# Residual update and next norm by halves of the tokens in a two-layer diffusion block

## The chip, the cores and the metric

One NeuronCore of a Trainium2 chip runs the whole program in one launch. The metric is device time in microseconds (us). TensorE is called PE below, VectorE DVE, ScalarE ACT, GpSimd POOL, and SP is the engine that issues most loads.

## The reference

Two layers (DEPTH = 2) act on 256 latent tokens `x` and 256 context tokens `ctx`, each 1024 wide, in float32. Each layer has three sublayers, and each of these takes the residual stream `h`, normalises it, applies a product, normalises the result and adds it:

```python
def modulate(x, g, shift, scale):
    return rms_norm(x, g) * (1.0 + scale) + shift

def ffn_sublayer(x, shift, scale, gate, g_pre, g_post, wg, wu, wd):
    y = swiglu(modulate(x, g_pre, shift, scale), wg, wu, wd)
    return x + FFN_RES * gate * rms_norm(y, g_post)
...
        h = ffn_sublayer(h, mod[:, 0], ...)          # and hc, with the context's own shift, scale, gate
        y, yc = token_mixing(modulate(h, g[2], ...), modulate(hc, g[2], ...), ...)
        h = h + mod[:, 5] * rms_norm(y, g[3])        # and hc, if another layer follows
        h = ffn_sublayer(h, mod[:, 6], ...)
```

`rms_norm` takes its mean over the 1024 features of one token, so a norm needs the whole of the residual of its tokens, but of no others. `D_FF` is 2816. `token_mixing` projects to 21 tiles of 128 columns, runs window attention, a gated linear attention (gla) and an mLSTM, and projects back with `w_out`.

## The kernel before

**Layout.** Features lie on the 128 partitions and tokens on the free axis: `H[128, 8, 512]` is the residual, with the latents in columns 0 to 255 of each of its KT = 8 feature tiles and the context in 256 to 511. The normed input is held as a high and a low part, `u_hi` and `u_lo`, the FFN's middle as `ht_hi` and `ht_lo`, the weights as `w_hi` and `w_lo`. `products` issues three matmuls for each product of two such pairs (L324, L325, L326), with up to 512 tokens each. In the second layer the part behind the mixer has latents alone, so all its operations have 256 tokens.

**Weights.** The weights come in 182 units, in the order of their use. Unit n uses slot n % 2 of `raw`, `w_hi` and `w_lo`. SP loads it, ACT writes `w_hi` (`split_hi`, L300, waits for the load and for `unit_used`: PE must be done with unit n-2), DVE writes `w_lo` (`split_lo`, L308), and PE waits for `lo_ready` (`begin`). A unit of gate and up weights holds 128 columns of each (48 products of 512 tokens). An output tile of `down` has two units of 11 feature blocks each, 33 products apiece; it is accumulated in bank 4 or 5 in turn. A unit of `project_out` holds two output tiles.

**Between two products.** There are five places where one sublayer ends and the next begins; z counts the sublayers from 0 to 5. At each, all of the following runs between the last product of one and the first of the next:
- ACT squares the last output tile (L724) and copies it with its gate to `Y_ffn` or `Y_mix` (L729, `post_tile`); the squares of the first seven tiles were added up by DVE (L1075).
- PE sums the squares over the partitions with a column of ones (L1617), ACT takes the root (L662), DVE the reciprocal (L984), PE spreads it over the partitions (L1624).
- DVE scales each tile of Y (L1086) and adds it to H (L1094), 8 tiles; ACT squares each new tile of H (L687), PE sums them (L1617), then root, reciprocal and spread again.
- for each of the 8 tiles DVE scales H (L1005), ACT applies the modulation (L696) and copies to `u_hi` (L700), DVE subtracts to `u_lo` (L1000), and PE's first unit of the next product takes tile k as soon as `u_ready` says so. In this stretch ACT and DVE also split the next product's second unit.

The order on each engine is that of the code: each engine's program is written out by hand, with semaphores between them. In three of the FFN products DVE also sums columns of a 512-wide matrix for later layers' modulation (`ada_sums`, L1025 and L1034), four instructions at a time, between its own steps.

## Time and profile before

| what | value |
|---|---|
| time, median of 3 runs (lowest, highest) | 2001.98 us (1999.55, 2007.71) |
| time of the profiled execution | 2008.94 us |
| its span, first to last instruction | 2007.1 us |
| PE busy with matmuls | 1873.5 us, 93% |
| DVE busy | 1109.3 us, 55% |
| ACT busy | 760.1 us, 38% |
| POOL busy | 243.6 us, 12% |
| mean granted clock of PE, share of full | 0.953 |

The profiled execution has 1.8 us around its span. PE is the busy engine, and its clock is at its full level (2.4 GHz) save for a few stretches at half of it (1.2 GHz). The places at which PE is not busy, and where its clock falls, are those between two products, and parts of the mixer. How busy an engine is on the whole tells little there: within such a place it matters which engine is waited for last.

### The profile page before, as it was taken

What the parts mean: (1) busy time and instruction counts of PE and PEld (TensorE: products, weight loads), DVE (VectorE), ACT (ScalarE), POOL (GpSimd) and SP (SyncE); (2) the same over time, 40 slices, a digit from 0 to 9 for tenths busy, and PEclk for the clock granted to TensorE, in tenths of its full rate; (3) what the DMA queues carried; (4) which work ended last, traced back from release to release, by engine and by line L of the source; (5) the groups of instructions that cost most, each with busy time, mean ns of one, the idle gap of its engine ahead of it and who ended that gap; (6) DMA issues with size and microseconds to landing.
All of it is one profiled execution on the core that took longest, in us unless ns stands there. A gap on an engine that the chain in (4) does not pass through costs nothing. (4 is left out here: it accounts for less than half of the span.)

```text
span 2007.1 us, 25666 instructions
## 1 busy us (share of the span) xinstructions
PE 1873.5 (93%) x10461; PEld 1521.9 (76%) x10461; DVE 1109.3 (55%) x1630; ACT 760.1 (38%) x1132; POOL 243.6 (12%) x327
## 2 busy tenths in 40 slices
PE   5999999979998886999999979999999799879998
PEld 3788877857786664888778858887888488769997
DVE  1777722245756646777522267775222676855544
ACT  4423222236436445222313253222232645654443
POOL 4011110012531000111110001110000152000000
PEclk7999999989999797999999979999999799979999
DMA  9566654342321022666553416665234243036654
GB/s 298 147 180 196 178 160 141 96 113 43 85 64 43 11 63 63 202 178 191 168 173 87 115 49 202 178 194 153 79 94 113 65 106 84 13 105 165 178 166 122
DMA packets 366469, 254.05 MB, mean 127 GB/s; under 512 B 30610, under 2 KB 343276, under 8 KB 366352
## 3 DMA queue, kind: packets, MB, share of 16 engines
q1 hardware_dynamic: 345648, 182.97, 33.1%
q0 software_dynamic: 20704, 69.44, 10.8%
q8 instruction: 83, 1.36, 0.3%
q14 instruction: 34, 0.28, 0.0%
HBM read 251.30 MB, written 1.07 MB: 126 GB/s over the span
## 5 line engine op out<-in xcount | busy, mean ns | idle before, releaser
L324 PE MATMUL bank<-u_hi,w_hi 128*128 128x512 f32 (+2 forms) x1872 | 690.8, 369 | 29.7 <-DVE u_lo L1000 20.6
L325 PE MATMUL bank<-u_lo,w_hi 128*128 128x512 f32 (+2 forms) x1872 | 682.8, 365 | 0.0
L326 PE MATMUL bank<-u_hi,w_lo 128*128 128x512 f32 (+2 forms) x1872 | 682.5, 365 | 0.0
L308 DVE TENSOR_TENSOR w_lo<-raw,w_hi 128x2048 fp32r<-128x2048 f32 (+2 forms) x182 | 373.0, 2049 | 262.3 <-ACT w_hi L300 262.1
L324 PEld LDWEIGHTS bank<-u_hi,w_hi 128*128 128x128 f32 (+1 forms) x1872 | 357.8, 191 | 110.8 <-issue 51.6
L326 PEld LDWEIGHTS bank<-u_hi,w_lo 128*128 128x128 f32 (+1 forms) x1872 | 357.5, 191 | 56.8 <-issue 0.9
L325 PEld LDWEIGHTS bank<-u_lo,w_hi 128*128 128x128 f32 (+1 forms) x1872 | 358.1, 191 | 53.8 <-issue 0.5
L300 ACT ACTIVATE w_hi<-raw 128x2048 fp32r<-128x2048 f32 (+2 forms) x182 | 311.8, 1713 | 144.0 <-PE bank L326 126.6
L324 PE MATMUL bank<-ht_hi,w_hi 128*128 128x512 f32 (+1 forms) x704 | 256.8, 365 | 1.4 <-DVE w_lo L308 1.4
L326 PE MATMUL bank<-ht_hi,w_lo 128*128 128x512 f32 (+1 forms) x704 | 255.3, 363 | 0.0
L325 PE MATMUL bank<-ht_lo,w_hi 128*128 128x512 f32 (+1 forms) x704 | 255.2, 363 | 0.0
L715 ACT ACTIVATE tmp_a<-bank 128x512 f32<-128x512 f32 (+1 forms) x88 | 47.9, 544 | 537.1 <-PE bank L326 537.1
L1034 DVE SCALAR_TENSOR_TENSOR ada_sum<-ada_slot,silu_c,ada_sum 128x512 f32<-128x512 f32 x336 | 230.7, 746 | 0.0
L512 POOL DMA_DIRECT2D ada_slot<-in_ada_w_dram x128 | 92.1, 720 | 936.3 <-DVE ada_sum L1034 655.1
L1053 DVE TENSOR_TENSOR tmp_b<-bank,tmp_a 128x512 f32<-128x512 f32 (+1 forms) x88 | 55.0, 625 | 210.9 <-ACT tmp_a L715 210.9
L324 PEld LDWEIGHTS bank<-ht_hi,w_hi 128*128 128x128 f32 x704 | 132.8, 189 | 27.6 <-issue 6.7
L326 PEld LDWEIGHTS bank<-ht_hi,w_lo 128*128 128x128 f32 x704 | 132.8, 189 | 20.7
L325 PEld LDWEIGHTS bank<-ht_lo,w_hi 128*128 128x128 f32 x704 | 132.9, 189 | 20.4
L724 ACT ACTIVATE tmp_a<-bank 128x512 f32<-128x512 f32 (+1 forms) x48 | 25.3, 527 | 206.6 <-PE bank L326 206.6
L1075 DVE TENSOR_TENSOR tmp_b<-tmp_b,tmp_a 128x512 f32<-128x512 f32 (+1 forms) x36 | 21.7, 604 | 124.0 <-ACT tmp_a L724 124.0
L1056 DVE TENSOR_TENSOR ht_lo<-tmp_b,ht_hi 128x512 fp32r<-128x512 f32 (+1 forms) x88 | 55.1, 626 | 56.7 <-ACT ht_hi L717 56.7
L717 ACT ACTIVATE ht_hi<-tmp_b 128x512 fp32r<-128x512 f32 (+1 forms) x88 | 50.9, 578 | 61.1 <-DVE tmp_b L1053 61.1
(244 smaller groups left out, 1486.4 us busy)
## 6 DMA issues: line engine op xcount, KB each, us to landing
ada_slot<-in_ada_w_dram POOLq DMA_DIRECT2D x128, 512.0 KB, 4.7
...
```

The lines of the kernel that those rows point to most:

```text
L300: nc.scalar.activation(w_hi[s][:, 0:size], raw[s][:, 0:size], ACT.Copy).then_inc(hi_ready[s], 1)
L308: nc.vector.tensor_tensor(w_lo[s][:, 0:size], raw[s][:, 0:size], w_hi[s][:, 0:size].bitcast(F32), ALU.subtract).then_inc(lo_ready[s], 1)
L324: nc.tensor.matmul(acc, wh, xh, start=first, stop=False)
L325: nc.tensor.matmul(acc, wh, xl, start=False, stop=False)
L326: return nc.tensor.matmul(acc, wl, xh, start=False, stop=last)
L512: pool.dma_start(ada_slot[slot][:], src[:, 2 * r:2 * r + 2, b * BLOCK:(b + 1) * BLOCK]).then_inc(ada_loaded[slot], 16)
L715: nc.scalar.activation(tmp_a[j][:, 0:T], bank[2 * j][:, 0:T], ACT.Silu).then_inc(gated["silu_ready"], 1)
L717: nc.scalar.activation(ht_hi[:, f, 0:T], tmp_b[j][:, 0:T], ACT.Copy).then_inc(gated["hthi_ready"], 1)
L724: nc.scalar.activation(tmp_a[b][:, 0:T], bank[4 + b][:, 0:T], ACT.Square).then_inc(post["ysq_ready"], 1)
L1034: ins = nc.vector.scalar_tensor_tensor(acc[:], ada_slot[slot][:, kk, :], c_k, acc[:], ALU.mult, ALU.add)
L1053: nc.vector.tensor_tensor(tmp_b[j][:, 0:T], bank[2 * j + 1][:, 0:T], tmp_a[j][:, 0:T], ALU.mult).then_inc(gated["prod_ready"], 1)
L1056: nc.vector.tensor_tensor(ht_lo[:, f, 0:T], tmp_b[j][:, 0:T], ht_hi[:, f, 0:T].bitcast(F32), ALU.subtract).then_inc(gated["ht_ready"], 1)
```

## The change

At the first four of the five places (z < HALVED = 4) the work is done for the latents first and then for the context, 256 tokens at a time, and PE's products are cut the same way and put between the steps:
- the last output tile of the sublayer (`last_tile`) is computed for the latents in bank 5, then for the context in bank 6. Between the context's products PE sums the latents' squares, spreads their reciprocal and sums the squares of their new H;
- the first two weight units of the next product (`halved_gate_up`, or four output tiles in `project`) are computed for the latents, then for the context, again with the context's sums between the products. In `project` the tiles 0 to 3 now use four banks;
- ACT and DVE have one sequence each for the whole place (`halved_norm`), in which the latents' norm and the context's residual update alternate (`last_half` squares and copies one half of the last tile, `half_root` takes a root, `u_part` waits for `u_ready`). The splits of the next product's units are placed within it: the first unit's split, which was in `down`, and the second's;
- at the end of `project_out`, ACT has a semaphore of its own for tile 6 (`six_done`).
The counts of the semaphores change with it (`posts`, `norms`); POOL's waits for `ss_done` now wait for the context's half. The work behind z = 4, for latents alone, stays as it was.

```diff
+            def halved_norm(z, Y, n_last):
+                layer, q = (z + 1) // 3, (z + 1) % 3
+                act.wait_ge(post["ysq_added"], (KT - 1) * z + KT - 2)
+                act.wait_ge(post["lat_done"], z + 1)
+                last_half(Y, z, 0)
+                half_root(POST_SUMS, 0, 0, post["ss_done"], post["ss_rms"], posts(z) + 1)
+                if z == 1:
+                    unit_done(act, n_last, 0, 2, 0)
+                    last_half(Y, z, 1)
+                for k in range(KT):
+                    if k == KT // 2 and z != 1:
+                        split_hi(act, second_unit(layer, q) - 1)
+                    half_square(z, 0, k)
+                if z != 1:
+                    unit_done(act, n_last, 0, 2, 0)
+                    last_half(Y, z, 1)
+                half_root(NORM_BANKS[0], 0, 1, norm["sq_used"], norm["rms_ready"], KT * norms(z + 1) + KT)
+                half_root(POST_SUMS, 1, 0, post["ss_done"], post["ss_rms"], posts(z, 1) + 1)
+                for k in range(KT):
+                    half_mod(z, 0, k)
+                    if k == KT // 2 + 1:
+                        split_hi(act, second_unit(layer, q))
+                    if k >= KT // 2:
+                        half_square(z, 1, k - KT // 2)
+                for k in range(KT // 2, KT):
+                    half_square(z, 1, k)
+                half_root(NORM_BANKS[1], 1, 1, norm["sq_used"], norm["rms_ready"], KT * norms(z + 1, 1) + KT)
+                for k in range(KT):
+                    half_mod(z, 1, k)
...
+                half_invert(0, 0, post["ss_rms"], posts(z) + 1, post["ss_rstd"])
+                dve.wait_ge(mod_done, max(MODS_BEFORE_POST[z], MODS_BEFORE[z + 1]))
+                dve.wait_ge(post["ss_spread"], posts(z) + 1)
+                y_scale(0, 0)
+                for k in range(KT):
+                    if k + 1 < KT:
+                        y_scale(0, k + 1)
+                    h_add(0, k)
+                if z != 1:
+                    split_lo(dve, second_unit(layer, q) - 1)
+                half_invert(0, 1, norm["rms_ready"], norms(z + 1) + 1, norm["rstd_ready"])
+                half_invert(1, 0, post["ss_rms"], posts(z, 1) + 1, post["ss_rstd"])
+                dve.wait_ge(norm["rstd_spread"], norms(z + 1) + 1)
+                for k in range(KT):
+                    u_scale(0, k)
+                    if k == 2:
+                        dve.wait_ge(post["ss_spread"], posts(z, 1) + 1)
+                    if k >= 1:
+                        low(0, k - 1)
+                    if k >= 2:
+                        y_scale(1, k - 2)
+                    if k >= 3:
+                        h_add(1, k - 3)
+                low(0, KT - 1)
+                split_lo(dve, second_unit(layer, q))
+                y_scale(1, KT - 2)
+                h_add(1, KT - 3)
+                y_scale(1, KT - 1)
+                h_add(1, KT - 2)
+                h_add(1, KT - 1)
+                half_invert(1, 1, norm["rms_ready"], norms(z + 1, 1) + 1, norm["rstd_ready"])
+                dve.wait_ge(norm["rstd_spread"], norms(z + 1, 1) + 1)
+                for k in range(KT):
+                    u_scale(1, k)
+                    if k >= 1:
+                        low(1, k - 1)
+                low(1, KT - 1)
...
+            def halved_gate_up(layer, q, g, z):
+                n0 = first_unit[f"gu{q}", layer]
+                def part(j, w, k, h):
+                    s = (n0 + j) % 2
+                    return products(bank[2 * j + w][:, HALF[h]], tile_of(w_hi[s], w * DM, k), tile_of(w_lo[s], w * DM, k),
+                                    u_hi[:, k, HALF[h]], u_lo[:, k, HALF[h]], k == 0, k == KT - 1)
+                begin(n0)
+                wait(pe, gated["prod_ready"], FT * g)
+                for k in range(KT):
+                    u_part(z, 0, k)
+                    for w in range(2):
+                        part(0, w, k, 0)
+                    if k >= 4:
+                        norm_sum(z - 1, 1, k - 4)
+                begin(n0 + 1)
+                for w in range(2):
+                    for k in range(KT):
+                        part(1, w, k, 0)
+                        n = w * KT + k
+                        if n in (1, 3, 5, 7):
+                            norm_sum(z - 1, 1, n // 2 + 4)
+                        if n == 11:
+                            norm_spread(z - 1, 1)
+                for k in range(KT):
+                    u_part(z, 1, k)
+                    for w in range(2):
+                        last = part(0, w, k, 1)
+                last.then_inc(unit_used[n0 % 2], 1)
+                for w in range(2):
+                    for k in range(KT):
+                        last = part(1, w, k, 1)
+                last.then_inc(unit_used[(n0 + 1) % 2], 1)
...
+                def last_tile():
+                    for j in range(2):
+                        begin(n0 + 2 * KT - 2 + j)
+                    for h in range(2):
+                        for f in range(FT):
+                            s, k = (n0 + f // half) % 2, f % half
+                            if h == 1 and f == 2:
+                                post_sums(z, 0)
+                            if h == 1 and f == 8:
+                                post_spread(z, 0)
+                            if h == 1 and f >= 13 and f % 2 == 1:
+                                norm_sum(z, 0, (f - 13) // 2)
+                            last = products(bank[LAST_BANKS[h]][:, HALF[h]], tile_of(w_hi[s], 0, k), tile_of(w_lo[s], 0, k),
+                                            ht_hi[:, f, HALF[h]], ht_lo[:, f, HALF[h]], f == 0, f == FT - 1)
+                            if h == 0 and f == FT - 1:
+                                last.then_inc(post["lat_done"], 1)
+                            elif h == 1 and k == half - 1:
+                                last.then_inc(unit_used[s], 1)
+                    for k in range((FT - 13 + 1) // 2, KT):
+                        norm_sum(z, 0, k)
+                    post_sums(z, 1)
+                    norm_spread(z, 0)
+                    post_spread(z, 1)
...
-                s = begin(n0)
+                def half_tile(t, k, h):
+                    s = (n0 + t // 2) % 2
+                    rows = P if t != T_SMALL else GATE_ROW + 4 * C_HEADS
+                    at = t % 2 * DM
+                    return products(proj_bank(t)[0:rows, HALF[h]], tile_of(w_hi[s], at, k)[:, 0:rows],
+                                    tile_of(w_lo[s], at, k)[:, 0:rows], u_hi[:, k, HALF[h]], u_lo[:, k, HALF[h]], k == 0, k == KT - 1)
+                begin(n0)
                 for k in range(KT):
-                    pe.wait_ge(norm["u_ready"], KT * z + k + 1)
-                    first = tile(0, k)
-                    last = tile(1, k)
-                    if k == KT - 1:
-                        first.then_inc(m["tile_done"], 1)
-                        last.then_inc(unit_used[s], 1)
-                for t in range(2, N_PROJ):
+                    u_part(z, 0, k)
+                    for t in range(2):
+                        half_tile(t, k, 0)
+                    if k >= 4:
+                        norm_sum(z - 1, 1, k - 4)
+                begin(n0 + 1)
+                ahead = [t for t in (3, 2) if T == TOK or t not in LAT_ONLY]
+                for t in ahead:
+                    for k in range(KT):
+                        half_tile(t, k, 0)
+                        if t == 3 and k % 2 == 1:
+                            norm_sum(z - 1, 1, k // 2 + 4)
+                        if t == 2 and k == 3:
+                            norm_spread(z - 1, 1)
+                if len(ahead) == 1:
+                    norm_spread(z - 1, 1)
+                for k in range(KT):
+                    u_part(z, 1, k)
+                    first = half_tile(0, k, 1)
+                    last = half_tile(1, k, 1)
+                first.then_inc(m["tile_done"], 1)
+                last.then_inc(unit_used[n0 % 2], 1)
+                for t in (2, 3):
+                    for k in range(KT):
+                        last = half_tile(t, k, 1 if t in ahead else 0)
+                    last.then_inc(m["tile_done"] if t == 2 else unit_used[(n0 + 1) % 2], 1)
+                gla_after(2, layer, m, z, T)
+                gla_after(3, layer, m, z, T)
+                for t in range(4, N_PROJ):
...
+                def last_tile(s):
+                    for h in range(2):
+                        for e, k in enumerate(OUT_ORDER):
+                            if h == 1 and e == 3:
+                                post_sums(z, 0)
+                            at = slice((2 * k + 1) * P, (2 * k + 2) * P)
+                            last = products(bank[LAST_BANKS[h]][:, HALF[h]], w_hi[s][:, at], w_lo[s][:, at],
+                                            u_hi[:, k, HALF[h]], u_lo[:, k, HALF[h]], e == 0, e == KT - 1)
+                        last.then_inc(unit_used[s] if h == 1 else post["lat_done"], 1)
+                    post_spread(z, 0)
+                    post_sums(z, 1)
+                    for k in range(KT):
+                        norm_sum(z, 0, k)
+                    norm_spread(z, 0)
+                    post_spread(z, 1)
                 pe.wait_ge(m["att_ready"], T // P)
                 for u in range(KT // 2):
                     s = begin(n0 + u)
                     for t in range(2 * u, 2 * u + 2):
-                        wait(pe, post["y_ready"], KT * z + t - 1)
+                        wait(pe, post["y_ready"], KT * z + min(z, HALVED) + t - 1)
+                        if z < HALVED and t == KT - 1:
+                            last.then_inc(post["six_done"], 1)
+                            last_tile(s)
+                            return
```

In the lists of instructions below, `w_hi0` and `w_hi1` are the two slots; the line numbers are each version's own (L324 to L326 became L339 to L341, L308 became L323).

**PE, last output tile of `down`, z = 0.** Before: the last product of tile 6 (bank 4), the tile's first unit, and further down its second.

```order
L326 MATMUL bank4<-ht_hi_79,w_lo1_55 128x512
L324 MATMUL bank5<-ht_hi_79,w_hi0_52 128x512 [waits lo_ready0,y_ready]
L325 MATMUL bank5<-ht_lo_80,w_hi0_52 128x512
L326 MATMUL bank5<-ht_hi_79,w_lo0_54 128x512
...
L324 MATMUL bank5<-ht_hi_79,w_hi1_53 128x512 [waits lo_ready1]
L325 MATMUL bank5<-ht_lo_80,w_hi1_53 128x512
```

With the change, from the same product of tile 6 on:

```order
L341 MATMUL bank4<-ht_hi_79,w_lo1_55 128x512
L339 MATMUL bank5<-ht_hi_79,w_hi0_52 128x256 [waits lo_ready1,lo_ready0,y_ready]
L340 MATMUL bank5<-ht_lo_80,w_hi0_52 128x256
...
L339 MATMUL bank6<-ht_hi_79,w_hi0_52 128x256
L340 MATMUL bank6<-ht_lo_80,w_hi0_52 128x256
...
L1816 MATMUL bank7<-tmp_b0_62,ones_66 32x128 [waits ysq_added]
L1816 MATMUL bank7<-tmp_b0_62,ones_66 32x128
L1816 MATMUL bank7<-tmp_a1_61,ones_66 32x128 [waits ysq_ready]
L1816 MATMUL bank7<-tmp_a1_61,ones_66 32x128
L339 MATMUL bank6<-ht_hi_79,w_hi0_52 128x256
```

The tile now runs through both units once for the latents and once for the context, with the latents' sums behind two feature blocks of the context; its first matmul waits for both slots, where it waited for slot 0, and the wait for slot 1 stood 33 products further down.

**ACT, the same place.** Before: tile 6 leaves bank 4, then the splits of the tile's second unit and of the next sublayer's first, then the last tile.

```order
L724 ACTIVATE tmp_a0_60<-bank4 128x512 [waits ysq_added,unit_used1]
L729 ACTIVATE Y_ffn_89<-bank4,mod0_68 128x256 x2
L300 ACTIVATE w_hi1_53<-raw1_51 128x1408 [waits unit_used1,raw_loaded1]
L300 ACTIVATE w_hi0_52<-raw0_50 128x2048 [waits unit_used0,raw_loaded0]
L724 ACTIVATE tmp_a1_61<-bank5 128x512 [waits ysq_added,unit_used1]
```

With the change:

```order
L751 ACTIVATE tmp_a0_60<-bank4 128x512 [waits ysq_added,unit_used1]
L756 ACTIVATE Y_ffn_89<-bank4,mod0_68 128x256 x2
L315 ACTIVATE w_hi1_53<-raw1_51 128x1408 [waits unit_used1,raw_loaded1]
L763 ACTIVATE tmp_a1_61<-bank5 128x256 [waits lat_done,ysq_added]
L764 ACTIVATE Y_ffn_89<-bank5,mod0_68 128x256
L770 ACTIVATE rstd_64<-bank7,eps_col_75 64x128 [waits ss_done]
L778 ACTIVATE tmp_a0_60<-H_49 128x256 [waits h_added]
...
L315 ACTIVATE w_hi0_52<-raw0_50 128x2048 [waits unit_used0,raw_loaded0]
```

The split of the tile's second unit stands where it stood, behind tile 6; that of the next sublayer's first unit moved behind the fourth square of the latents' new H.

**DVE, z = 0, where the latents' norm meets the context's update.** Before, the last addition to H, the split of the second unit, the reciprocal, then a scaling (L1005, reads H) and a subtraction (L1000, writes `u_lo`) of 512 tokens in turn:

```order
L1094 TENSOR_TENSOR H_49<-H_49,tmp_b1_63 128x512 [waits y_scaled]
L308 TENSOR_TENSOR w_lo1_55<-raw1_51,w_hi1_53 128x2048 [waits hi_ready1]
L984 RECIPROCAL rstd_64<-rstd_64 128x128 [waits rms_ready]
L1005 TENSOR_TENSOR tmp_b0_62<-H_49,bank5 128x512 [waits u_ready,rstd_spread,mod_done]
L1005 TENSOR_TENSOR tmp_b1_63<-H_49,bank5 128x512 [waits u_ready]
L1000 TENSOR_TENSOR u_lo_78<-tmp_b0_62,u_hi_77 128x512 [waits uhi_ready]
```

With the change (L1220 is the scaling, L1225 the subtraction, both of the latents; L1209 scales the context's Y, L1214 adds it to H):

```order
L1220 TENSOR_TENSOR tmp_b0_62<-H_49,bank4 128x256 [waits u_ready]
L1225 TENSOR_TENSOR u_lo_78<-tmp_b1_63,u_hi_77 128x256 [waits uhi_ready]
L1209 TENSOR_TENSOR tmp_b0_62<-Y_ffn_89,bank6 128x256 [waits h_added]
L1214 TENSOR_TENSOR H_49<-H_49,tmp_b1_63 128x256 [waits y_scaled]
L1220 TENSOR_TENSOR tmp_b1_63<-H_49,bank4 128x256 [waits u_ready]
L1225 TENSOR_TENSOR u_lo_78<-tmp_b0_62,u_hi_77 128x256 [waits uhi_ready]
```

Each feature tile of the latents' `u` now has four instructions of 256 tokens on DVE where it had two of 512.

## Rows read from the trace of the kernel before

**Rows 1.** The page: busy time of PE, and its granted clock in 40 slices.

```profile
PE 1873.5 (93%) x10461; PEld 1521.9 (76%) x10461; DVE 1109.3 (55%) x1630; ACT 760.1 (38%) x1132; POOL 243.6 (12%) x327
...
PEclk7999999989999797999999979999999799979999
```

**Rows 2.** Busy times between products at z = 0, 1, 2, 3.

```profile
core 0: us, PE busy (x) PEld busy (x) DVE busy (x) ACT busy (x) POOL busy (x), PEclk, DMA share, GB/s
427.90:451.50 23.60, 9.37 (x98) 4.69 (x96) 16.38 (x23) 11.13 (x19) 8.76 (x17) 0.58 0.48 116
758.20:783.40 25.20, 9.83 (x98) 5.09 (x96) 17.07 (x24) 12.34 (x22) 1.55 (x2) 0.59 0.28 84
1158.90:1183.00 24.10, 9.89 (x98) 5.20 (x96) 16.36 (x23) 11.11 (x19) 0.00 (x0) 0.57 0.26 69
1553.80:1577.20 23.40, 9.19 (x97) 4.68 (x96) 16.36 (x23) 11.11 (x19) 8.74 (x17) 0.59 0.47 117
```

**Rows 3.** Timeline, last output tile of `down` at z = 2: start, us, engine.

```profile
1144.05 0.39 PE L324 MATMUL bank<-ht_hi,w_hi 128*128 128x512 f32 x1
...
1144.25 0.60 ACT L724 ACTIVATE tmp_a<-bank 128x512 f32<-128x512 f32 x1 [6.04 <-PE bank L326]
...
1145.45 1.39 ACT L300 ACTIVATE w_hi<-raw 128x1408 fp32r<-128x1408 f32 x1
...
1146.88 1.63 DVE L308 TENSOR_TENSOR w_lo<-raw,w_hi 128x1408 fp32r<-128x1408 f32 x1 [1.31 <-ACT w_hi L300]
...
1158.78 0.39 PE L326 MATMUL bank<-ht_hi,w_lo 128*128 128x512 f32 x1
```

**Rows 4.** Timeline at z = 4, whose operations have 256 tokens.

```profile
1784.16 0.75 DVE L1086 TENSOR_TENSOR tmp_b<-Y_mix,bank 128x256 f32<-128x256 f32 x2 [1.12 <-PE bank L1624]
...
1789.59 0.75 DVE L1094 TENSOR_TENSOR H<-H,tmp_b 128x256 f32<-128x256 f32 x2
...
1790.40 2.29 DVE L308 TENSOR_TENSOR w_lo<-raw,w_hi 128x2048 fp32r<-128x2048 f32 x1
...
1793.45 0.94 DVE L984 RECIPROCAL rstd<-rstd 64x128 f32<-64x128 f32 x1 [0.76 <-ACT rstd L662]
...
1796.22 0.60 ACT L696 ACTIVATE tmp_b<-tmp_b,mod 128x256 f32<-128x256 f32 x1 [2.81 <-DVE tmp_b L1005]
1796.85 0.42 ACT L700 ACTIVATE u_hi<-tmp_b 128x256 fp32r<-128x256 f32 x1
...
1797.30 0.42 DVE L1000 TENSOR_TENSOR u_lo<-tmp_b,u_hi 128x256 fp32r<-128x256 f32 x1 [0.78 <-ACT u_hi L700]
```

**Rows 5.** Timeline, PE on products of 256 tokens: two at full clock, two at half.

```profile
1775.73 0.28 PE L325 MATMUL bank<-u_lo,w_hi 128*128 128x256 f32 x1
...
1779.81 0.28 PE L326 MATMUL bank<-u_hi,w_lo 128*128 128x256 f32 x1
...
1799.08 0.41 PE L326 MATMUL bank<-u_hi,w_lo 128*128 128x256 f32 x1
...
1801.43 0.41 PE L325 MATMUL bank<-u_lo,w_hi 128*128 128x256 f32 x1
```

**Rows 6.** Timeline behind the first unit of gate and up at z = 3.

```profile
1196.22 0.60 ACT L715 ACTIVATE tmp_a<-bank 128x512 f32<-128x512 f32 x1 [1.19 <-PE bank L326]
...
1200.97 2.28 DVE L308 TENSOR_TENSOR w_lo<-raw,w_hi 128x2048 fp32r<-128x2048 f32 x1
...
1206.93 0.39 PE L324 MATMUL bank<-u_hi,w_hi 128*128 128x512 f32 x1
```

**Rows 7.** Busy times in short stretches of `project`, second layer; the clock stands behind POOL's.

```profile
1599.00:1599.25 0.25, 0.25 (x2) 0.21 (x1) 0.25 (x1) 0.25 (x1) 0.00 (x0) 0.65 1.33 226
...
1602.25:1602.50 0.25, 0.25 (x2) 0.15 (x2) 0.00 (x0) 0.23 (x2) 0.00 (x0) 0.53 0.00 0
```

**Rows 8.** Timeline of `project`, first layer: the gla's chain up to its second level.

```profile
470.47 1.12 PE L1736 MATMUL bank<-proj,w_alpha 32*128 32x512 f32 x2
...
489.12 0.61 POOL L584 TENSOR_TENSOR gla_x<-gla_cum 128x256 f32<-128x256 f32 x1
...
493.23 1.06 ACT L789 ACTIVATE gla_x<-gla_x 128x1024 f32<-128x1024 f32 x1
...
504.95 0.68 DVE L1395 TENSOR_TENSOR gla_kq<-proj,gla_x 128x512 f32<-128x512 f32 x1
...
505.73 1.17 PE L1766 MATMUL bank<-gla_kq 32*128 32x128 f32 x32 [1.41 <-issue]
```

207 lines of the change are left out of this document (160 added, 47 removed).

## Prediction, before the changed kernel had run

> **What bounds the kernel now.** I read the page first: PE is busy 93% of the span, and its granted clock dips in some slices only [rows 1]. A change to work between products can gain only where PE is idle or slow, so the second view is the busy times of the stretches from the last product of one sublayer to the first of the next [rows 2]. There are four that the change touches, of 23.4 to 25.2 us. PE is busy 9.2 to 9.9 us in each, DVE 16.4 to 17.1, and the granted clock is 0.57 to 0.59: if the level is full and then half, it was full for (0.58 - 0.5) / 0.5 x 24 = 3.8 us, so it falls about 3.8 us after the last product. What sets the end of such a stretch is the chain from square through DVE's updates of H to the first `u`. The third view is the timeline at z = 4, where all this already runs on 256 tokens: it prices the half forms.
>
> **The prices.**
> - PE at 512 tokens: the last tile of `down` has 66 products and starts at 1144.05, its last matmul at 1158.78, 0.2266 each [rows 3]. At 256 tokens and full clock 34 steps from 1775.73 to 1779.81, 0.120 each; at half clock 11 steps from 1799.08 to 1801.43, 0.214 [rows 5]. I take 0.1225 for a half product, as some wait for weights. (A product here is one matmul; three of them make one product of pairs.)
> - DVE at 256 tokens: from the first scaling of Y at 1784.16 to the end of the last addition 1790.34 is 6.2 us for 8 pairs; `split_lo` 2.29; a reciprocal 0.94; `u_lo` 0.42. ACT: modulation 0.60, `u_hi` 0.42 [rows 4]. A scaling of 256 tokens is 0.38 (0.75 for two).
>
> The clock's answer to new pauses has no such row; part 2 bounds it.
>
> **Part 1, the last output tile's new wait: +4.45 us, three times.** `last_tile` in `down` calls `begin` for both units ahead of its first matmul. The second unit goes to slot 1, which PE frees only with the last product of tile 6, so ACT and DVE can't split it earlier. The timeline at z = 2 shows how long that takes [rows 3]: tile 6 ends at 1144.05, ACT squares it (1144.25), copies it, splits at 1145.45 (1.39), DVE follows at 1146.88 (1.63), done at 1148.51. That is 4.45 us after the tile's start. Before, PE spent these on the first unit's 33 products (7.5 us) and the wait was hidden. Now nothing covers it: PE has no other work queued, and ACT and DVE keep their order there. It occurs at z = 0, 2 and 3 (at z = 1 the last two tiles are in one unit that is ready): 3 x 4.45 = **+13.35 us**.
>
> **Part 2, the clock after that wait: 0 to 1.7 us each, 1.0 taken.** The pause of 4.45 us is a little longer than the 3.8 us after which the clock falls in [rows 2]. The shortest low spell that I found lasts from 1599.0, where a quarter microsecond reads 0.65, to 1602.3, where it reads 0.53 and rises: 3.3 us, with PE busy in both [rows 7]. In a low spell each microsecond of 256-token work does 1 - 0.120 / 0.214 = 0.44 us less. So 0 if the clock stays up, 3.9 x 0.44 = 1.7 if it falls at the end and must rise again. I take 1.0, nearer to the upper end: **+3.0 us**, range 0 to 5.
>
> The Trainium skill, "TensorE: Matmul & The Clock Gate", Part 1, describes the low level as TensorE's default, which only activity lifts. By it halved products with gaps between them could stay at the low level, which is the third rival below, worked out there from rows.
>
> **Part 3, the place itself.** I wrote down the order of PE, ACT and DVE and gave each step its price. L is the end of the latents' half of the last tile.
> - (a) To the latents' spread: PE still has the context's products, 24 half ones until the sums (2.9), sums 0.5, spread 0.8: L + 4.2.
> - (b) 8 pairs of scaling Y and adding: 6.2, L + 10.4.
> - (c) `split_lo` of the next sublayer's first unit, which stood in `down` before: 2.25, L + 12.65.
> - (d) two reciprocals: 1.9, L + 14.6 (the second one is of the context's square sum, and stands ahead of the latents' first scaling).
> - (e) first `u`: 0.38 + 0.60 + 0.42 + 0.42 and handovers, 2.0, L + 16.6.
> - (f) seven more tiles. DVE has four instructions for each (scale H, subtract, scale the context's Y, add), 4 x 0.38 = 1.5, against PE's 6 matmuls (0.73) and 0.25 of sums: DVE sets the pace, 7 x 1.5 = 10.5, L + 27.1.
> - (g) the second unit's split 2.25 and five half instructions 1.9, L + 31.3.
> - (h) the context's last square, PE's sums between the second unit's products, root, reciprocal, spread: 4.4, L + 35.7.
> - (i) the context's `u`: 2.0 for the first, then 7 x 0.98 (ACT's two instructions), L + 44.6.
> - (j) six matmuls, 0.7: the first unit is used at L + 45.3. The second unit's context half (48 matmuls, 5.9) ends at 51.2.
> - (k) the third unit. At z = 2 its slot was freed just before ACT's 1196.22, and its `w_lo` was done at 1200.97 + 2.28 = 1203.25, since DVE's `ada_sums` stand ahead [rows 6]. That is 7.25 after the first unit's end. Now PE gets there after 5.9, so it waits 1.4: third unit at L + 52.6, with handovers **L + 53.0**.
>
> Before, at z = 2: the tile starts at 1144.05 [rows 3], its first half's worth of work (66 x 0.1225) would end at 1152.15 = L, and the third unit began at 1206.93 [rows 6], L + 54.8. So the whole reordering brings **1.8 us** there, not the third of the stretch that the idle PE suggests: PE does get the latents' products in early, at L + 17 in place of 1183.0 = L + 30.9, but the context's `u`, which the third unit needs as well, ends no earlier, as DVE does 64 half instructions where it did 32 full ones, and each split is the same length and now stands on the chain.
>
> At z = 1 there is no step (c), so L + 50.7 to 51.7 for the third unit. Before: products end at 758.2, L is 2.9 - 0.4 earlier, 755.8; the next begin at 783.4 [rows 2] and the third unit 23.9 later, as at z = 2: 807.3, L + 51.5. I put **0.2 us lost**.
>
> At z = 0 and 3 `project` follows. PE's `z_mm` stood at 470.47 [rows 8]; L is 427.9 - 14.95 + 8.1 = 421.05 there, so L + 49.4. Tiles 0 to 3 now all come before it; by the sum above they end at L + 51.2, with a wait 51.7: 2.3 later. What follows isn't bound by PE: from z_mm to the gla's second level at 504.95 DVE, POOL and ACT are waited for (PE idles 1.41 us ahead of L1766) [rows 8]. In it ACT's exponential at 493.23 stands behind the copy of a projected tile, though POOL had its input at 489.7, 3.5 earlier. With one tile more ahead of z_mm that copy comes a tile sooner. Up to 3.5 is gained, less a little I take 3.1: **0.8 us gained** at each. The bounds are -1.2 (all 3.5) and +2.3 (none).
>
> Sum of part 3: -1.8 + 0.2 - 0.8 - 0.8 = **-3.2 us**. The added matmul issue is in it: 0.120 x 2 against 0.2266 is 0.014 for a pair, for 66 + 96 = 162 pairs 2.3 us per place, all of it inside the L + 51 of PE, which isn't last before step (k). The Trainium skill, same page, section "Back-to-back issue gap", gives N / 2.4 + 2.5 ns: 109 ns for 256 columns and 216 for 512, 2 ns for a pair; the rows say 14. By the page the 2.3 us would be 0.3. It changes no sum.
>
> **Other edits.** POOL's clears wait for the context's half of `ss_done` instead of the whole; they come some 8 us later and are needed only at z_mm: 0. SP's loads keep their order, and their slots are freed by the same last products: 0. Copies and squares of the last tile by halves: a few 0.1 us on ACT, beside PE's work.
>
> **Sum.** +13.35 + 3.0 - 3.2 = **+13.2 us**: the profiled 2008.94 would be 2022.1, the median 2002.0 would be **2015**. The two differ by 0.35%, within the spread of the three runs, and I assume the difference carries over.
>
> **The rivals.**
> 1. *The latents' products fill the gap (faster).* Were DVE's pace in (f) not the bound, so that the context's chain ran beside PE at PE's price, each place would lose the idle PE time but for the chain to L + 17: third unit around 10 us earlier. 4 x -10 + 13.35 = -27, **1975 us**. It decides at DVE's work per feature tile, 1.5 us against PE's 0.98; and (g) to (i) must shrink too. For it: PE is idle for over 14 us of each stretch [rows 2]. Against: each DVE price is read in [rows 4]. 0.07.
> 2. *Part 1 as said, without its clock, and part 3 twice as good (same).* 13.35 - 6.4 = +7, **2009 us**. If ACT runs ahead in (i) or the reciprocals overlap the spread. 0.16.
> 3. *The clock stays low over the halved products.* In (f) PE works 0.98 of every 1.5 us and has room even at the low level; what counts is the second unit and the third's start, some 6.6 us of work at 0.44: 2.9 x 4 = +11.6, **2027 us**. For it: the low spell of [rows 7] came with PE busy. 0.17.
> 4. *Something else is late* (a split behind a square that waits, in each place, 5 us): 2035. 0.04.
>
> **How the numbers follow.** Forecast 0.56, own range 2011 to 2021 (clock 0 to 5, part 3 from -7 to +1). Range for 8 in 10: 2007 to 2029, which leaves out rival 1, rival 4 and the tails. A measurement of this kernel can tell about 0.5%, 10 us, from no change. Above 2012: most of the forecast (0.53 of its 0.56), rivals 3 and 4 (0.21) and the upper end of rival 2 (0.04): 0.78. Within: 0.16. Below 1992: rival 1 in the main, 0.06.
>
> **What the profile will show.** Step 1: ahead of the last tile's first matmul at z = 0, 2, 3 PE idle for 4.4 to 4.6 us, released by DVE's `w_lo`; if it is under 1 us the sum falls by 13. Part 2: the granted clock at half for 3 to 4 us around there. Part 3: first latents' product at L + 17 (rather than 20 or more), DVE's pace 1.5 us for a feature tile in (f), a wait of 1 to 2 us on `w_lo` ahead of the third unit. The forecast is wrong if PE starts the third unit at L + 45, or if the clock is low in the second unit.

## The result: 1.2% slower, and the profile after

| | before | with the change |
|---|---|---|
| median (lowest, highest) | 2002.13 us (1999.55, 2007.71) | 2027.03 us (2025.85, 2027.87) |
| ratio to before, 95% interval | | 1.012 (1.0098 to 1.0142) |
| span of the profiled execution | 2007.1 us | 2026.1 us |
| mean granted clock | 0.953 | 0.970 |

The forecast was 2015 with a range of 2007 to 2029. Sign and range hold, the latter with 2 us to spare; the loss is 24.9 us where 13.2 were forecast.

The page after: busy times, and the granted clock in 40 slices, beside [rows 1].

```profile
PE 1899.9 (94%) x11043; PEld 1563.4 (77%) x11043; DVE 1126.0 (56%) x1766; ACT 778.0 (38%) x1208; POOL 243.7 (12%) x327
...
PEclk8999999999999998999999999999999999989999
```

PE is busier and its clock is on average higher, and yet it takes longer: the clock was low before where PE had little to do, and the idle time has moved. The timeline at z = 2 (start, us, engine) shows where. First the last tile of `down`, beside [rows 3]:

```profile
1146.19 0.60 ACT L751 ACTIVATE tmp_a<-bank 128x512 f32<-128x512 f32 x1 [6.04 <-PE bank L341]
1146.68 0.83 ACT L756 ACTIVATE Y_ffn<-bank,mod 128x256 f32<-128x256 f32 x2
1147.39 1.38 ACT L315 ACTIVATE w_hi<-raw 128x1408 fp32r<-128x1408 f32 x1
1148.81 1.62 DVE L323 TENSOR_TENSOR w_lo<-raw,w_hi 128x1408 fp32r<-128x1408 f32 x1 [1.30 <-ACT w_hi L315]
...
1150.58 0.49 PE L339 MATMUL bank<-ht_hi,w_hi 128*128 128x256 f32 x1 [4.43 <-DVE w_lo L323]
```

PE has been idle for 4.43 us and was released by DVE's `w_lo`, as step 1 said; the same row with 4.43 stands at 417.02 (z = 0) and 1551.99 (z = 3). The busy times around it (of z = 2, the pause and what follows it, then the pause of z = 3):

```profile
core 0: us, PE busy (x) PEld busy (x) DVE busy (x) ACT busy (x) POOL busy (x), PEclk, DMA share, GB/s
1146.10:1150.60 4.50, 0.07 (x2) 0.05 (x1) 2.31 (x2) 2.59 (x4) 0.00 (x0) 1.00 0.15 36
1150.60:1154.30 3.70, 3.70 (x18) 3.70 (x19) 0.00 (x0) 0.00 (x0) 0.00 (x0) 0.54 0.71 204
1547.50:1552.00 4.50, 0.07 (x2) 0.04 (x1) 2.32 (x2) 2.59 (x4) 0.00 (x0) 0.78 0.08 24
```

At z = 2 the clock falls to its half level at the end of the pause, and nearly all of PE's first 3.7 us of products run at it (0.54 on the mean); at z = 3 it falls within the pause (0.78). Now the rest of the place, in the order of my steps:

```profile
1160.33 0.38 ACT L763 ACTIVATE tmp_a<-bank 128x256 f32<-128x256 f32 x1 [11.55 <-PE bank L341]
...
1164.59 0.75 DVE L1209 TENSOR_TENSOR tmp_b<-Y_ffn,bank 128x256 f32<-128x256 f32 x2 [1.70 <-PE bank L1824]
...
1170.67 2.29 DVE L323 TENSOR_TENSOR w_lo<-raw,w_hi 128x2048 fp32r<-128x2048 f32 x1
1174.14 1.76 DVE L1200 RECIPROCAL rstd<-rstd 64x128 f32<-64x128 f32 x2 [1.18 <-ACT rstd L770]
...
1178.00 0.55 PE L339 MATMUL bank<-u_hi,w_hi 128*128 128x256 f32 x1 [1.33 <-DVE u_lo L1225]
...
1187.94 2.28 DVE L323 TENSOR_TENSOR w_lo<-raw,w_hi 128x2048 fp32r<-128x2048 f32 x1
...
1191.27 0.75 DVE L1214 TENSOR_TENSOR H<-H,tmp_b 128x256 f32<-128x256 f32 x2
...
1193.53 0.42 ACT L778 ACTIVATE tmp_a<-H 128x256 f32<-128x256 f32 x1 [0.82 <-PE bank L1816]
1195.51 0.41 PE L1816 MATMUL bank<-tmp_a,ones 128*32 128x128 f32 x4
1195.96 0.36 ACT L770 ACTIVATE rstd<-bank,eps_col 64x128 f32<-64x128 f32 x1 [2.02 <-PE bank L1816]
...
1197.47 0.71 PE L1824 MATMUL bank<-rstd,ident 64*128 64x128 f32 x4
1198.21 0.75 DVE L1220 TENSOR_TENSOR tmp_b<-H,bank 128x256 f32<-128x256 f32 x2 [0.91 <-PE bank L1824]
...
1215.26 0.50 PE L339 MATMUL bank<-u_hi,w_hi 128*128 128x512 f32 x1 [1.37 <-DVE w_lo L323]
```

The end of the latents' half, L, is 1160.2. Before, PE stood idle until 1183.07 at this place; now it starts on the next product at 1178.00, 17.8 us after L. But the third unit starts at 1215.26 = L + 55.1, where before it was L + 54.8: counted from L, the reordering brings nothing here, and the pause and the clock in the last tile, which lie ahead of L, come on top.

**Reading place by place.** One more profile of the kernel before (run e0) lets the places be told apart. In both versions I take the time of the same instruction behind each place and subtract: z = 0 up to the last tiles of `project_out`, z = 1 and z = 2 up to the eighth silu behind, z = 3 up to the second layer's last FFN. These differences are worked out from the timelines' starts, in us against e0:

| place | before, first profile | after | e1 | e2 | e3 | e4 | e8 | e5 | e6 | e7 | e9 |
|---|---|---|---|---|---|---|---|---|---|---|---|
| z = 0 | (+6.8) | +6.7 | +0.9 | +6.0 | +11.0 | -0.8 | 0.0 | (+8.0) | +0.4 | (+7.2) | (+4.4) |
| z = 1 | -1.2 | +1.5 | +1.5 | +0.9 | +1.4 | -2.1 | 0.0 | +0.2 | +0.2 | +0.2 | -3.8 |
| z = 2 | +0.1 | +6.6 | +0.5 | +4.0 | +8.5 | -2.4 | -0.3 | 0.0 | 0.0 | -0.1 | -4.2 |
| z = 3 | +0.6 | +10.2 | +4.4 | +8.3 | +12.7 | +0.7 | +3.6 | +4.3 | +3.2 | +3.5 | -2.8 |

The numbers in brackets hold a low-clock spell of the mixer, told next. The first column is the same kernel as e0, so one profile against another moves a place by up to 1.2 us without any edit; a single difference below that isn't shown by this table. The column "after" sums to 25.0, close to the difference of the medians, 24.9; the forecast had 4.7, 0.2, 3.7 and 4.7.

### The profile page after: what moved, and what is told of

Its sections match the earlier page's. It is cut to its first block and busy times, and to the rows that moved or that the text cites. A ratio compares the mean times of both kernels' runs of the same rounds, so it can differ in the third digit from the quotient of the medians.

```text
span 2026.1 us, 27070 instructions
## 1 busy us (share of the span) xinstructions
PE 1899.9 (94%) x11043; PEld 1563.4 (77%) x11043; DVE 1126.0 (56%) x1766; ACT 778.0 (38%) x1208; POOL 243.7 (12%) x327
## 5 line engine op out<-in xcount | busy, mean ns | idle before, releaser
L339 PE MATMUL bank<-u_hi,w_hi 128*128 128x512 f32 (+2 forms) x2000 | 720.6, 360 | 34.7 <-DVE u_lo L1225 12.7
L340 PE MATMUL bank<-u_lo,w_hi 128*128 128x512 f32 (+2 forms) x2000 | 706.6, 353 | 0.0
L341 PE MATMUL bank<-u_hi,w_lo 128*128 128x512 f32 (+2 forms) x2000 | 705.5, 353 | 0.0
L323 DVE TENSOR_TENSOR w_lo<-raw,w_hi 128x2048 fp32r<-128x2048 f32 (+2 forms) x182 | 372.8, 2048 | 246.7 <-ACT w_hi L315 246.5
L339 PEld LDWEIGHTS bank<-u_hi,w_hi 128*128 128x128 f32 (+1 forms) x2000 | 383.0, 191 | 123.3 <-issue 44.7
L341 PEld LDWEIGHTS bank<-u_hi,w_lo 128*128 128x128 f32 (+1 forms) x2000 | 383.2, 192 | 50.0
L340 PEld LDWEIGHTS bank<-u_lo,w_hi 128*128 128x128 f32 (+1 forms) x2000 | 383.6, 192 | 47.6
L339 PE MATMUL bank<-ht_hi,w_hi 128*128 128x512 f32 (+1 forms) x770 | 273.4, 355 | 15.6 <-DVE w_lo L323 15.6
L341 PE MATMUL bank<-ht_hi,w_lo 128*128 128x512 f32 (+1 forms) x770 | 268.9, 349 | 0.0
L339 PEld LDWEIGHTS bank<-ht_hi,w_hi 128*128 128x128 f32 x770 | 148.0, 192 | 44.1 <-issue 23.2
L341 PEld LDWEIGHTS bank<-ht_hi,w_lo 128*128 128x128 f32 x770 | 148.0, 192 | 18.3
L340 PEld LDWEIGHTS bank<-ht_lo,w_hi 128*128 128x128 f32 x770 | 148.3, 193 | 17.8
## 6 DMA issues: line engine op xcount, KB each, us to landing
ada_first<-in_ada_w_dram SPq DMA_DIRECT2D x4, 2048.0 KB, 14.6
```

Of the source, the lines that this page charges most:

```text
L323: nc.vector.tensor_tensor(w_lo[s][:, 0:size], raw[s][:, 0:size], w_hi[s][:, 0:size].bitcast(F32), ALU.subtract).then_inc(lo_ready[s], 1)
L339: nc.tensor.matmul(acc, wh, xh, start=first, stop=False)
L340: nc.tensor.matmul(acc, wh, xl, start=False, stop=False)
L341: return nc.tensor.matmul(acc, wl, xh, start=False, stop=last)
```

## The experiments

Each ratio below is to runs of the kernel before taken beside the experiment. Their median was 2005 to 2006 us there, and not the 2002.13 of the table above.

**e0, the kernel before once more.** No edit.

> The kernel before, unchanged, to see its mixer once more. In the profile of before the granted clock is at half from 681 to 701 us, in the first layer's mixer, and in the profile of the changed kernel it is not; PE's way from there to the mixer's last step took 8 us less. Theory (that spell comes and goes from execution to execution and is no part of the change): in this profile it may be missing, then the span is 1999 to 2001 us, and the time from z = 0's products to those of z = 1 is 8 us shorter than in the first profile. Rival (it belongs to the kernel before, and the change removed it): the spell is there again, and the span is 2005 to 2008.

Measured: one run, 2001.9 us, span 2000.1, 7 us under the first profile. The busy times of PE in the first layer's mixer, first profile and then this one:

```profile
681.00:701.00 20.00, 20.00 (x93) 16.23 (x94) 8.30 (x29) 5.05 (x14) 0.00 (x0) 0.50 0.01 1
```

```profile
673.50:693.50 20.00, 16.67 (x158) 13.12 (x156) 14.35 (x50) 10.98 (x34) 0.00 (x0) 1.00 0.01 1
```

The same kernel did this work once at half clock for 20 us and once at full clock. The spell is no property of either version (the profiles of e5, e7 and e9 had it too). So the difference of the two first spans, 19.0 us, hides some 7 us of the loss, and one profile of each would have misled by a quarter.

**e1, the pause taken away.**

```diff
-                    for j in range(2):
-                        begin(n0 + 2 * KT - 2 + j)
+                    begin(n0 + 2 * KT - 2)
                     for h in range(2):
                         for f in range(FT):
+                            if h == 0 and f == half:
+                                begin(n0 + 2 * KT - 1)
```

> The last tile of down waits for its first unit alone; the wait for the second unit stands ahead of the latents' twelfth feature block. Nothing else is changed. Theory (the pause of 4.43 us at z = 0, 2, 3 is on the path, and the clock's fall that follows it costs 1.7 us more): the second unit is ready 4.45 us after tile 6 ends, PE reaches it after 33 x 0.1225 = 4.04, so 0.4 us of wait is left, and no low spell: 3 x (4.43 - 0.4 + 1.7) = 17.2 us less than the changed kernel, 2010 us, ratio to before 1.004. Rival 1 (the low spell is there anyhow, since the products are half as wide): 3 x 4.0 = 12 us less, 2015, ratio 1.0065, and half clock in the last tile. Rival 2 (the pause hides behind the chain of DVE and ACT that follows): under 5 us less, ratio over 1.010.

Measured: 2009.95 us, ratio to before 1.0026 (1.0007 to 1.0045). The wait that is left, and the busy times of the last tile, z = 2:

```profile
1145.45 0.39 PE L339 MATMUL bank<-ht_hi,w_hi 128*128 128x256 f32 x1 [0.40 <-DVE w_lo L323]
```

```profile
1141.00:1149.60 8.60, 8.20 (x68) 8.00 (x67) 2.32 (x2) 2.60 (x4) 0.00 (x0) 1.00 0.45 123
```

0.40 us of wait, full clock throughout. Against after, z = 0, 2 and 3 lose 5.8, 6.1 and 5.8 us of cost, z = 1 none: 17.7, where 17.2 was expected. So the pause with its clock is some 17 of the 25 us, and it is one line's doing: a wait for a unit 33 products before its first use.

**e2, a shorter pause.** In `down`, ACT and DVE split the last tile's second unit before they square, copy and add tile 6:

```diff
-                            if z >= HALVED or 4 * i + ahead < 2 * KT:
+                            if z >= HALVED or 4 * i + ahead < 2 * KT - 1:
                                 ahead_of(split_hi, act, n0, i, 4, ahead)
+                        if z < HALVED and 2 * i + t == KT - 2:
+                            split_hi(act, n0 + 2 * KT - 1)
```

and the same with `split_lo` on DVE.

> ACT and DVE split the last tile's second unit ahead of squaring, copying and adding tile 6; the wait stays where the change put it. Theory (the clock falls some 3.8 us after PE stops): the pause shrinks by ACT's square and copy, 1.2 us, to 3.2 us, too short for a fall: 3 x (1.2 + 1.7) = 8.7 us less than the changed kernel, and the granted clock stays full in the last tile. Rival (any such pause brings a low spell): 3 x 1.2 = 3.6 us less, with half clock for 3 to 4 us behind each pause.

Measured: one run, 2021.0 us, 6.0 less than after, between theory and rival. The pause is 3.28 us at all three places (to 415.89 at z = 0). The stretch around it at z = 2, and the one behind it at z = 0:

```profile
1142.50:1150.50 8.00, 4.72 (x31) 4.02 (x30) 2.23 (x2) 2.59 (x4) 0.00 (x0) 1.00 0.54 150
415.90:420.00 4.10, 4.10 (x22) 4.10 (x23) 0.44 (x1) 0.00 (x0) 0.00 (x0) 0.58 0.83 222
```

At z = 2 the clock stayed up and the place cost 2.6 us less, near the 2.9 of my theory; at z = 0 the same pause was followed by a low spell, and 0.7 was saved. At z = 3 the clock fell as well (0.8 us before PE's restart), and 1.9 was saved. Neither expectation holds for all places: the length of a pause alone doesn't decide whether the clock falls. What does is open.

**e3, a longer pause.** DVE writes the low part of the last tile's second unit twice (a semaphore of its own between the two).

> DVE writes the low part of the last tile's second unit twice, one behind the other, at z = 0, 2, 3: the pause is longer by one such instruction, 1.6 us. Theory (the pause stands on the path at its full length, and the low spell behind it lasts as long whatever the pause): pauses of 6.0 to 6.1 us, 3 x 1.65 = 5 us more than the changed kernel, a low spell of 3.5 us in the last tile as before. Rival 1 (the pause is partly hidden): under 2 us more. Rival 2 (the low spell grows with the pause): 3 x (1.65 + 0.7) = 7 us more.

Measured: one run, 2036.8 us; pauses of 6.09 us. Against after, z = 0 costs 4.3 more, z = 2 1.9, z = 3 2.4, 8.6 in all. None is under the 1.65 of added pause, so nothing behind it is seen to absorb a pause. Up to L alone the three take 2.7, 2.4 and 1.6 us more: beyond the pause that is clock, as PE's products at half clock last 5.6 us in place of 3.2 at z = 0, 5.1 in place of 3.5 at z = 2, and 4.6 in place of 4.8 at z = 3. The other 1.6 at z = 0 come later, where e3 has low spells from 486 to 493 and from 517 to 521, and after one from 485 to 488. The total is beyond rival 2's number, but the spell didn't grow at all places.

**e4, the context's sums first.** On top of e1. In `halved_gate_up` (and so in `project`):

```diff
+                for k in range(4, KT):
+                    norm_sum(z - 1, 1, k)
                 begin(n0 + 1)
-                for w in range(2):
-                    for k in range(KT):
-                        part(1, w, k, 0)
-                        n = w * KT + k
-                        if n in (1, 3, 5, 7):
-                            norm_sum(z - 1, 1, n // 2 + 4)
-                        if n == 11:
-                            norm_spread(z - 1, 1)
+                rest = [(w, k) for w in range(2) for k in range(KT)]
+                for w, k in rest[0:3]:
+                    part(1, w, k, 0)
+                norm_spread(z - 1, 1)
+                for w, k in rest[3:8]:
+                    part(1, w, k, 0)
...
+                    part(1, *rest[8 + k], 0)
```

The last line stands behind the context's product k, so eight of the latents' products of the second unit are moved there as well. On DVE `split_lo` of the second unit moves from ahead of the context's last five half instructions to behind them.

> On top of e1_late_begin. PE sums the last four context squares right behind the latents' first unit, not between products of the second unit, and spreads the reciprocal after three of these; DVE does the context's last five half instructions ahead of the second unit's split, not behind it. Theory (in my step (h) the context's sums queue behind PE's products, 1.25 us apart, and the split of 2.3 us stands ahead of the last additions, both on the chain to the context's u): the context's u starts some 4 us sooner at each of the four places; the third unit is then bound by the end of the first unit plus 7.3, 3 us sooner at z = 1 and 2, and z_mm 3 us sooner at z = 0 and 3, of which 2 to 3 come through. 9 to 12 us less than e1: 1999, ratio to before 0.995 to 0.998. Rival (PE's total work sets the end, sums waiting ahead of products only idle it): within 3 us of e1, 2008, ratio 1.002.

Measured: 1999.34 us, ratio to before 0.9976 (0.9955 to 0.9997). The four places gain 1.7, 3.6, 2.9 and 3.7 us against e1, 11.9 in all, the upper end of the theory's 9 to 12. In its timeline at z = 2 the last sum, its root and the context's first scaling:

```profile
1174.10 0.41 PE L1816 MATMUL bank<-tmp_a,ones 128*32 128x128 f32 x4 [0.27 <-ACT tmp_a L778]
1174.56 0.36 ACT L770 ACTIVATE rstd<-bank,eps_col 64x128 f32<-64x128 f32 x1 [0.51 <-PE bank L1816]
...
1177.23 0.75 DVE L1220 TENSOR_TENSOR tmp_b<-H,bank 128x256 f32<-128x256 f32 x2 [1.22 <-PE bank L1824]
```

The scaling comes 16.1 us after the latents' first product (1161.13); after the change it was 20.2 (1198.21 - 1178.00). From the end of the last addition to that of the spread it is 4.2 us at each of the four places.

**e8, PE's part of e4 alone.** DVE's order as the change has it.

> e4_sums_first with PE's part alone: PE sums the last four context squares right behind the latents' first unit; DVE keeps the second unit's split ahead of the context's last five half instructions. Theory (both stand on the chain: PE's queue costs 2 us of it, the split of 2.3 us the rest): the context's u comes some 2 us later than in e4 and 2 us sooner than in e1 at each place, 1.5 to 2 us a place in the end: 6 to 8 us more than e4 if one leaves aside low-clock spells in the mixer, read place by place from the trace. Rival (PE's order was all): within 1 us a place of e4.

Measured: one run, 2004.9 us. Place by place it lies between e1 and e4: 0.9, 1.5, 0.9 and 0.8 better than e1, 0.8, 2.1, 2.1 and 2.9 worse than e4. Both parts count: PE's order for about 4 us of the 12, 1 a place where the theory had 2, and DVE's split for about 8. The single differences are of the size of what one profile differs from another, so it is the sums, and the same sign at all four places, that carry this. What the sums alone and the eight moved products are each worth within PE's part wasn't tried.

**e5, the context's reciprocal later.** On top of e4:

```diff
                 half_invert(0, 1, norm["rms_ready"], norms(z + 1) + 1, norm["rstd_ready"])
-                half_invert(1, 0, post["ss_rms"], posts(z, 1) + 1, post["ss_rstd"])
                 dve.wait_ge(norm["rstd_spread"], norms(z + 1) + 1)
                 for k in range(KT):
                     u_scale(0, k)
+                    if k == 1:
+                        half_invert(1, 0, post["ss_rms"], posts(z, 1) + 1, post["ss_rstd"])
```

and PE's `post_spread(z, 1)` behind the latents' first products.

> On top of e4_sums_first. The context's reciprocal of the residual norm stands behind the latents' second scaling on DVE, and its spread behind the latents' first products on PE. Theory (step (d): two reciprocals in a row put 0.88 us on the chain to the latents' first u): the first product of the latents comes 0.9 us sooner at each place, and all behind it, since DVE and ACT are the chain: 4 x 0.9 = 3.6 us less than e4. Rival (the 0.88 comes back as the hole that it fills is not a hole): no difference over 1 us.

Measured: one run, 2012.8 us, with the mixer's spell in it; z = 1, 2 and 3 are 2.3, 2.4 and 3.7 us worse than e4, worked out as in the table. DVE at z = 2:

```profile
1168.56 0.75 DVE L1220 TENSOR_TENSOR tmp_b<-H,bank 128x256 f32<-128x256 f32 x2 [0.80 <-PE bank L1825]
1169.23 0.94 DVE L1200 RECIPROCAL rstd<-rstd 64x128 f32<-64x128 f32 x1
...
1173.48 0.42 DVE L1225 TENSOR_TENSOR u_lo<-tmp_b,u_hi 128x256 fp32r<-128x256 f32 x1 [2.50 <-PE bank L1825]
```

Without the second reciprocal in front, DVE waits 0.80 us for PE's spread, and its first scaling comes 1.74 us behind the start of the first reciprocal (1166.82), as late as with both in a row (1.75, from 1174.14 to 1175.89 after the change): a hole had hidden it. Moved, it stands between the first scalings and the first subtraction, and the second subtraction then waits 2.50 us for the spread. Step (d) had the wrong reason, and even the rival was too kind.

**e6, the third unit's split first.** On top of e5, at z = 1 and 2:

```diff
+                        if 0 < 3 * layer + 2 * q <= HALVED and f < 2:
+                            if f == 0:
+                                split_hi(act, n0 + 2)
-                        if f > 0 or layer + q == 0:
+                        elif f > 0 or layer + q == 0:
                             ahead_of(split_hi, act, n0, i, 2, j + 1)
```

and the same with `split_lo` on DVE.

> On top of e5_reciprocal. At z = 2 and 3 of the gate and up products (the places z = 1 and 2), ACT and DVE split the third unit ahead of the first unit's silu, product and column sums. Theory (step (k): 7.3 us from the first unit's end to the third's weights, of which ACT's table load, silu and copy and DVE's sums are 3): the wait ahead of the third unit goes, 2 to 3 us less at each of the two places: 4 to 6 us less than e5, 1992 to 1995 us, ratio to before 0.992 to 0.995. Rival (PE is not waiting for it once the context's u is the bound, or the late silu holds back the fourth unit): no gain over 1 us against e5.

Measured: 2009.1 us, the median of nine of ten runs, ratio to before 1.0019 (1.0002 to 1.0037). The tenth took 3733.9 us, and no trace here tells why. z = 1 and z = 2 stand where e5 has them (0.2 and 0.2, 0.0 and 0.0). PE's wait has moved one unit on:

```profile
1212.90 0.50 PE L339 MATMUL bank<-u_hi,w_hi 128*128 128x512 f32 x1 [0.97 <-DVE w_lo L323]
```

This is the fourth unit; its split now waits behind the sums of columns that the third's had waited for. The rival is right.

**e7, a narrow context update.** On top of e1, DVE's scaling of Y and addition to H have 8 columns for the context; its other 248 tokens keep their old residual.

> On top of e1_late_begin. Left out: DVE scales and adds 8 of the context's 256 tokens only, at all four places (the rest of the context's residual stays as it was), so that two of DVE's four instructions per feature tile cost next to nothing. Theory of the prediction (in step (f) DVE sets the pace with four instructions, 1.5 us a tile, against ACT's 1.0): the latents' eight tiles take 8 us instead of 10.2, and step (g) 1.5 less: 3.5 us less at each place, 14 us less than e1. Rival (ACT, with modulation, copy, squares and the split of 1.9, is the bound as well): the eight tiles still take 9.5 to 10 us, the gain is step (g) alone, 4 x 1.5 = 6 us.

Measured: one run, 2013.4 us, with the mixer's spell. z = 1, 2 and 3 are 1.3, 0.6 and 0.9 better than e1, far from 3.5, and under the rival's 1.5. At z = 2:

```profile
1176.96 1.90 ACT L315 ACTIVATE w_hi<-raw 128x2048 fp32r<-128x2048 f32 x1
...
1180.14 0.42 DVE L1227 TENSOR_TENSOR u_lo<-tmp_b,u_hi 128x256 fp32r<-128x256 f32 x1 [2.14 <-ACT u_hi L789]
...
1189.18 0.36 ACT L770 ACTIVATE rstd<-bank,eps_col 64x128 f32<-64x128 f32 x1 [2.02 <-PE bank L1818]
```

DVE has time now and waits 2.14 us for ACT, which is splitting the second unit; and the root still waits 2.02 us for PE's sums, whatever DVE saved in step (g). In (f) ACT was as much the bound as DVE, and (h) was PE's.

**e9, one ACT instruction less for each tile of u.** On top of e4:

```diff
...
-                nc.scalar.activation(part, part, ACT.Identity, bias=mod[layer][:, 3 * q, k, h:h + 1],
-                                     scale=mod[layer][:, 3 * q + 1, k, h:h + 1]).then_inc(norm["moded"], 1)
-                act.wait_ge(norm["moded"], at)
-                nc.scalar.activation(u_hi[:, k, HALF[h]], part, ACT.Copy).then_inc(norm["uhi_ready"], 1)
+                nc.scalar.activation(u_hi[:, k, HALF[h]], tmp_b[k % 2][:, HALF[h]], ACT.Identity,
+                                     bias=mod[layer][:, 3 * q, k, h:h + 1]).then_inc(norm["uhi_ready"], 1)
```

DVE's scaling becomes (H x scale) x reciprocal, its subtraction (tmp + shift) - u_hi.

> On top of e4_sums_first. At the four places DVE scales H by the reciprocal and by the modulation's scale in one instruction, ACT adds the shift while it writes u_hi, and DVE adds the shift again while it subtracts: ACT has one instruction of 0.42 us for each tile of u where it had two of 1.0 together. Theory (after e7: ACT is the pace of the u in both halves, 1.0 us a tile, and DVE's four instructions 1.4): the latents' eight tiles are no longer held by ACT but by DVE, 1.4 to 1.6 us a tile, 0 to 1 us less; the first u comes 0.6 us sooner; the context's tiles come at DVE's 0.8 us in place of 1.0, 1.5 us less. 2 to 3 us less at each place, 8 to 12 us less than e4: 1989, ratio to before 0.991 to 0.994. Rival (PE's work behind the context's first u, 0.36 x 3 a tile, is the bound by now): 1 us a place, 4 us in all, ratio 0.996.

Measured: 1996.02 us, ratio to before 0.9938 (0.9916 to 0.9961), the fastest version of this study. Of its seven runs three took 1987.2 to 1987.7 us and four 1996.0 to 1999.6; the profile is of one of the four, and the two groups differ by about what the mixer's spell costs. z = 1, 2 and 3 gain 1.8, 1.8 and 3.5 us against e4. Up to 1.5 of the 3.5 may be clock: a low spell late in that mixer lasts 3.4 us here and 6.8 in e4. z = 0 can't be read to its end, as the spell lies in it. The context's tiles at z = 2, first two of eight:

```profile
1180.35 0.48 DVE L1222 SCALAR_TENSOR_TENSOR u_lo<-tmp_b,mod,u_hi 128x256 fp32r<-128x256 f32 x1 [0.19 <-ACT u_hi L784]
1180.87 0.48 DVE L1216 SCALAR_TENSOR_TENSOR tmp_b<-H,mod,bank 128x256 f32<-128x256 f32 x1
1181.27 0.48 DVE L1222 SCALAR_TENSOR_TENSOR u_lo<-tmp_b,mod,u_hi 128x256 fp32r<-128x256 f32 x1
```

A tile takes 0.92 us where it took 1.0, with DVE's instructions at 0.48 us each in place of 0.42 and hardly a wait between them. At z = 1 and 2 the gain is just under the theory's 2 to 3 us a place, and the ratio is just within its 0.991 to 0.994; the three shortest runs are 2 us under its 1989.

## Why the prediction was right, and where its sizes were off

The direction and half of the loss come from part 1, which was right in mechanism and size. The other two parts together were forecast at -0.2 us and measured at +11.7. That the time still lies in the range of 2007 to 2029 is owed to the width of that range: the forecast's own, 2011 to 2021, was missed (its terms, 0 and -7 us, would put its lower end at 2008, not 2011).

- **Part 1, the pause: right.** 4.45 us forecast, 4.43 measured, at the three places named, with the releaser named. e1 shows that it is on the path in full.
- **Part 2, its clock: mis-sized.** 1.0 us each was taken. PE's products ran at half clock for 3.2 us at z = 0, 3.5 at z = 2 and 4.8 at z = 3, where the clock fell within the pause already and stayed low to 1556.8. At 0.44 us lost in each that makes 1.4, 1.5 and 2.1. The measured times agree: from tile 6 to L, after takes 5.4, 5.5 and 6.2 us more than e1, 4.03 of it the wait. That is 5.0 in all against 3.0, and over my upper end of 1.7 at z = 3. So the price was right and the length wrong: the 3.9 us behind that upper end stand in no row (the row shows 3.3), and the 3.8 us from PE's stop to the fall of the clock are no constant. They were 4.2, 4.5 and 2.4 in the changed kernel. From e1, which took 3 x 4.03 us of wait away and gained 17.7, the clock's whole share is 5.6; 0.6 of it lies behind L.
- **Part 3, the reordering: the wrong sign.** -3.2 forecast, +6.1 measured in e1 (7.3 less the 1.2 us of waits left in it). With 13.3 for the pauses and 5.6 for the clock this makes the 25.0. By steps, counted from L, at z = 2: (a) to (c) 12.75 for 12.65; (d) 15.7 for 14.6, since the latents' root came 1.2 us after DVE was free, behind PE's sums (1.6 at z = 1, where no split stands between); (f) 10.2 for 10.5, though DVE's instruction took 0.33 us in a row without a wait and not 0.38, because ACT's split of 1.9 us filled the difference. (h) is the step that failed: 4.4 forecast from the last addition to the spread, 6.2 measured. I had priced the four sums as if PE were free for them; they are queued in its program, two products apart, and ACT's squares wait for them in turn [1193.53, 0.82 us], and then the root for the last one [1195.96, 2.02 us]. In e1, with the clock full, these waits are the same and (h) is 5.6, so 0.6 of the 1.8 us goes with the clock and 1.2 with the queue. With the sums moved (e4) it is 4.2. (j) and (k) carry (h) on: L + 55.1 for 53.0.
- **z = 3: the largest error,** +4.4 in e1 for -0.8. z_mm came 5.4 us late (2.3 forecast) and the chain to the second level gave 3.0 of it back, as forecast, which leaves 2.5. Part of the 5.4 is a row used for the wrong place: the prediction took z_mm's distance at z = 0 for both, but at z = 3 it stood nearer to the last tile in the kernel before, by 2.4 us in the first profile and 1.4 in e0. The rest, 1.8, goes with a low spell near the end of that mixer that was twice as long as in e0 (1743 to 1750 against 1738 to 1741), of which I can't say whether the change causes it.
- **Rival 1 (faster, because DVE keeps up): refuted,** and for a reason that stands nowhere in the prediction: e7 took half of DVE's instructions in (f) down to 8 columns and gained 0.6 to 1.3 us a place. The chain there is ACT's and PE's as well.
- **Rival 2 (half clock costs nothing, gains doubled): refuted** by e1.
- **Rival 3 (clock low over the halved products) gave 2027, the measured time, by another road.** The prediction would also call itself wrong if the clock was low in the second unit, and it was, at z = 0, 1 and 2 (454.3 to 457.7, 782.0 to 785.4, 1188.2 to 1191.6):

```profile
1188.20:1191.60 3.40, 3.35 (x16) 2.67 (x16) 3.37 (x5) 0.83 (x2) 0.00 (x0) 0.50 0.03 6
```

But the price is small. (h) takes 6.1 to 6.2 us where such a spell lies just ahead of it, and 5.5 to 5.6 where none does (z = 3, and z = 0, 2 and 3 in e1); at z = 2 the third unit starts at L + 55.1 with it and at L + 54.5 without. That is 0.6 us, where 2.9 was the rival's price. The rival's mechanism is there, at a fifth of its size; the number fits by chance.
